# 160 instead of 128 of 512 tokens of an expert layer by rows fetched by index: PE stages of 352 columns, first one-hots on GpSimd

## What is computed

```python
qry = (tb @ w_q).reshape(128, 8, 2, 128)          # tb: RMS-normed tokens
s = einsum('thpd,pkd->thpk', qry, sub_keys)       # 2 x 128 keys
...                                               # top 16 of 16*16 sums, per head
eidx = take_along_axis(cidx, pos)                 # 16 of 16384 experts for each of 8 heads
gates = softmax(top)
z = einsum('thed,td->the', expert_u[eidx], tb)
act = gates * gelu(z)
out = einsum('the,thed->td', act, expert_v[eidx])
```

## Time and profile before

| | us |
|---|---|
| three runs | 4529.89, 4532.38, 4532.43 |
| median | 4532.38 |
| the profiled execution, whole | 4528.72 |
| its span, first to last instruction | 4527.2 |
| PE busy in it | 4451.7 (98%) |
| DVE busy | 3336.6 (74%) |
| DMA, mean | 281 GB/s |

### The profile page before, as it was taken

The page is one execution under the profiler, slowest core; times in us unless marked ns, Lnnn a source line. Parts: engine busy times, 40 slices in busy tenths (PEclk is TensorE's granted clock), DMA queues, the critical chain, the costliest instruction groups (busy, mean ns, idle before and its releaser), DMA issues.

```text
span 4527.2 us, 66430 instructions
## 1 busy us (share of the span) xinstructions
PE 4451.7 (98%) x24985; PEld 4089.4 (90%) x24985; DVE 3336.6 (74%) x4048; ACT 1301.7 (29%) x1217; POOL 712.1 (16%) x742
## 2 busy tenths in 40 slices
PE   8999999999999999999899999999999999999998
PEld 6788878999999788878799999999999999999998
DVE  5767675988888645558878888777746788887886
ACT  4222222222222331222123444322223222322223
POOL 1111111010101200111111112233311111111113
PEclk9999999999999999999999999999999999999999
DMA  6988986888888968898446777898876888888884
GB/s 214 320 288 291 314 280 229 288 286 290 286 289 287 332 229 286 286 322 311 151 141 238 294 287 281 308 354 332 332 262 238 314 319 293 315 316 301 307 290 149
DMA packets 390000, 1272.99 MB, mean 281 GB/s; under 512 B 28288, under 2 KB 204304, under 8 KB 282272
## 3 DMA queue, kind: packets, MB, share of 16 engines
q1 hardware_dynamic: 335872, 940.51, 60.5%
q0 software_dynamic: 54048, 331.51, 19.6%
HBM read 1070.46 MB, written 335.61 MB: 311 GB/s over the span
## 4 chain that ended last, share of the span: by engine, by line
PE 83%; DVE 6%; DMA 5%; issue 3%; SPq 2%; ACT 1%; POOL 1%; DVEq 0%; POOLq 0%; ACTq 0%
PE bank L757 26%; PE bank L758 26%; PE bank L759 26%; DMA u_rows<-u_turned_b 2%; PE bank L981 2%; DMA u_rows<-u_turned_c 1%; SPq L402 1%; DVE w_lo L1424 1%; PE bank L857 1%; DVE u_turned_b L1431 1%; PE bank L864 1%; ACT w_hi L1047 1%; DVE u_turned_c L1431 1%; PE bank L833 1%; POOL cand L674 1%
## 5 line engine op out<-in xcount | busy, mean ns | idle before, releaser
L757 PE MATMUL bank<-x_hi,w_hi 128*128 128x384 f32 (+2 forms) x5760 | 1973.5, 343 | 27.0 <-DVE w_lo L1424 19.7
L758 PE MATMUL bank<-x_lo,w_hi 128*128 128x384 f32 (+2 forms) x5760 | 1966.6, 341 | 0.0
L759 PE MATMUL bank<-x_hi,w_lo 128*128 128x384 f32 (+2 forms) x5760 | 1958.0, 340 | 0.0
L1047 ACT ACTIVATE w_hi<-w_raw 128x2048 fp32r<-128x2048 f32 x432 | 827.2, 1915 | 1859.8 <-PE bank L759 1808.8
L1424 DVE TENSOR_TENSOR w_lo<-w_raw,w_hi 128x2048 fp32r<-128x2048 f32 x432 | 996.0, 2305 | 450.4 <-ACT w_hi L1047 448.1
L757 PEld LDWEIGHTS bank<-x_hi,w_hi 128*128 128x128 f32 x5760 | 1084.6, 188 | 131.9 <-issue 39.2
L759 PEld LDWEIGHTS bank<-x_hi,w_lo 128*128 128x128 f32 x5760 | 1087.6, 189 | 82.4
L758 PEld LDWEIGHTS bank<-x_lo,w_hi 128*128 128x128 f32 x5760 | 1085.2, 188 | 84.7 <-issue 2.6
L757 PE MATMUL bank<-x_hi_o,w_hi 128*128 128x384 f32 x2048 | 684.4, 334 | 0.7 <-DVE w_lo L1424 0.5
L758 PE MATMUL bank<-x_lo_o,w_hi 128*128 128x384 f32 x2048 | 684.1, 334 | 0.0
L759 PE MATMUL bank<-x_hi_o,w_lo 128*128 128x384 f32 x2048 | 684.1, 334 | 0.0
(11 more groups left out here) (284 smaller groups left out, 2726.8 us busy)
## 6 DMA issues: line engine op xcount, KB each, us to landing
v_rows<-v_blocks SPq DMA_DIRECT2D x128, 1024.0 KB, 10.4
w_raw<-u_blocks SPq DMA_DIRECT2D x128, 1024.0 KB
w_raw<-v_blocks SPq DMA_DIRECT2D x128, 1024.0 KB
w_raw<-w_proj SPq DMA_DIRECT2D x112, 1024.0 KB
u_raw_a<-u_blocks SPq DMA_DIRECT2D x99, 1024.0 KB, 8.3
u_rows<-u_turned_a SPq DMA_DIRECT2D x396, 256.0 KB, 5.7
z_scratch<-z_stage POOLq DMA_DIRECT2D x128, 192.0 KB
g_scratch<-g_chunk SPq DMA_DIRECT2D x12, 2048.0 KB, 12.1
```

Source lines behind the costliest of these rows:

```text
L757: pe.matmul(dst, whi, xhi, start=start, stop=False)
L758: pe.matmul(dst, whi, xlo, start=False, stop=False)
L759: return pe.matmul(dst, wlo, xhi, start=False, stop=stop)
L1047: act.activation(WH[s][:, :], RAW[s][:, :], ACT.Copy).then_inc(w_hi, 1)
```

## The change

- The first NT = 352 tokens go densely (N3 = 384 keeps the size of everything else). Every matmul of the U and V stages has 352 columns. z_stage, g, z_group and x_hi_o, x_lo_o shrink likewise. G needs 44 blocks (Z_GATE = 44) instead of 48.
- Tokens 352 to 383 go by pairs too. Their 32 x 128 pairs are laid over the partitions in four groups: partition 32 g + t holds pairs 32 g to 32 g + 31 of token t. So 32 more fetches and dots (ZIX, XRX, ZPX), and 32 more fetches and adds (VIX, GSX), ahead of the old 128: 160 in all (PAIRS).
- Their set-up: 16 more scalings on ACT and 16 transposes on PE in the Q and U stages (X_AT, take_x), an index computation of 12 instructions and a copy (rsX) on DVE ahead of the last table look-up, 12 small DMAs on POOL that spread the indices and gates over the partitions, one more transpose, one more GELU.
- In the V stage the four partial sums of a token have to be added: the first 32 adds are done by block 24, then behind block 25 PE multiplies ACC with a 0/1 matrix sel (16 matmuls, `x_flush`), DVE clears ACC and adds the result to out_sums (`x_flushed`), and the other 128 adds follow over blocks 26 to 119.
- hot_i is made by POOL, as four tensor_scalar of 128 elements for each group (`hot_rows`), with its own semaphore hot_i_rdy. In POOL's order a block's z store comes first, then the next block's hot_rows, then the u_rows.
- dots: 70 over the 44 gate blocks, 90 over the next 62 (to block 121). SP's wait for the last dot stands in front of the last 2 weight blocks instead of the last 8. The Python loops of DVE and POOL are written out.

```diff
-Z_LOOK, Z_GATE, TOK = 16, 48, 8
+Z_LOOK, Z_GATE, TOK = 16, 44, 8
...
-NT = TG * P
+N3 = TG * P
+NX = 32
+XG = P // NX
+XP = P // XG
+NT = N3 - NX
+PAIRS = XP + P
...
-V_FIRST, V_LAST = 1, 119
+X_FIRST, X_LAST, V_FIRST, V_LAST = 1, 24, 26, 119
+X_FLUSH = 25
...
-D_GATE, D_LATE = 9, 9
+D_GATE, D_LAST = 70, NB_E - 7
...
         def dots(n):
+            g = Z_LOOK + Z_GATE
+            upto = lambda m: (D_GATE * (m - Z_LOOK) // Z_GATE if m <= g else
+                              min(PAIRS, D_GATE + (PAIRS - D_GATE) * (m - g) // (D_LAST + 1 - g)))
+            return range(upto(n), upto(n + 1))
...
-            with sp.Fori(0, 26) as i:
+            g_chunk(NT // CH // 2, 0)
+            with sp.Fori(0, 31) as i:
                 z_load(Z_LOOK + 4 + Z_GATE + 2 * i)
...
-            sp.wait_ge(ug_dot, P)
+            sp.wait_ge(ug_dot, PAIRS)
             group_load(sp, 1, 1, zg_first, gg_first)
...
-            with sp.Fori(0, 4) as i:
-                z_load(Z_LOOK + 4 + Z_GATE + 52 + 2 * i)
+            z_load(NB_E - 2)
...
+            def hot_rows(n):
+                for g in range(2):
+                    pool.wait_ge(g_mm, 2 * n + (g + 1))
+                    pool.sem_inc(turns[1], 1)
+                    for q in range(4):
+                        tok = TOK * n + 4 * g + q
+                        o = pool.tensor_scalar(hot_i[g][:, q, :], iota[:, :], IT[:, tok:tok + 1], None, ALU.is_equal)
+                    o.then_inc(hot_i_rdy, 1)
...
+            pool.wait_ge(xi_rdy, 2)
+            for g in range(XG):
+                to, at_ = slice(NX * g, NX * g + NX), slice(XP * g, XP * g + XP)
+                pool.dma_start(ZIX[to, :], ZIT[P - NX:P, at_]).then_inc(xi_ld, 16)
+                pool.dma_start(VIX[to, :], VIT[P - NX:P, at_]).then_inc(xi_ld, 16)
+                pool.dma_start(GSX[to, :], GA[P - NX:P, TG - 1, at_]).then_inc(xi_ld, 16)
...
             for n in range(Z_LOOK, NB_E):
                 z_stores(n)
+                if n + 1 < Z_LOOK + Z_GATE:
+                    hot_rows(n + 1 - Z_LOOK)
                 for p in dots(n):
-                    if p + VSLOT < P:
+                    if p + VSLOT < PAIRS:
                         pool.wait_ge(ug_dot, p + 1)
                         u_row(p + VSLOT)
...
                         pe.wait_ge(hot_rdy, 4 * i + 2 * u + g + 1)
+                        pe.wait_ge(hot_i_rdy, 4 * i + 2 * u + g + 1)
...
+            def x_flush():
+                pe.wait_ge(vg_use, v_uses(XP - 1) + 1)
+                pe.wait_ge(sel_rdy, XG - 1)
+                for k in range(KT):
+                    m = pe.matmul(A[1][:, NX * k:NX * k + NX], ACC[:, P * k:P * k + P], sel[:], start=k == 0, stop=k == KT - 1,
+                                  skip_group_check=True)
+                m.then_inc(ax_rdy, 1)
...
-                        dve.tensor_tensor(hot_i[g][:, :, :], iota[:, :].unsqueeze(1).to_broadcast((P, 4, P)),
-                                          IT[:, ds(TOK * n + 4 * g, 4)].unsqueeze(2).to_broadcast((P, 4, P)), ALU.is_equal)
...
+            def x_flushed():
+
+                dve.wait_ge(ax_rdy, 1)
+                dve.memset(ACC[:, :], 0.0).then_inc(vg_use, 1)
+                o = OUT[:, :, NT:N3]
+                dve.tensor_tensor(o, A[1][:, :].rearrange("p (k t) -> p k t", k=KT), o, ALU.add).then_inc(ax_add, 1)
```

More of the change, by code:

```diff
@@ L225, in encoder_block @@
     HG = place("h_rows", [P, KT, P], F32, r1 + 8 * GJ * NT)
[L226 removed]
+    (OUT, ACC), e13 = lay(r2, [("out_sums", [P, KT, N3], F32), ("v_sums", [P, D], F32)])
     assert e13 <= dd
@@ L530, in _ @@
                       allow_small_or_imprecise_dtypes=True).then_inc(pool_const, 1)
+            pool.wait_ge(pool_const, 3)
+            pool.tensor_tensor(sel[:], ident[:, 0:NX], ident[:, NX:2 * NX], ALU.add).then_inc(sel_rdy, 1)
+            for g in range(2, XG):
+                pool.wait_ge(sel_rdy, g - 1)
+                pool.tensor_tensor(sel[:], sel[:], ident[:, NX * g:NX * g + NX], ALU.add).then_inc(sel_rdy, 1)
             pool.wait_ge(g_row, 2)
@@ L1011, in out_group @@
                         out_block(16 * gg + 8 * par + 2 * m_ + u, u, par)
-            with pe.Fori(0, KEYS // GJ // 2 - 1) as gg:
+            def x_flush():
[5 more added lines that the diff above has]
+                m.then_inc(ax_rdy, 1)
+            for g in range(4):
+                if g < X_FLUSH // 8:
+                    out_group(g // 2, g % 2)
+                else:
+                    pe.wait_ge(x_lo, 80 + 8 * g + 8)
+                    pe.sem_inc(turns[2], 1)
+                    for r in range(8):
+                        out_block(8 * g + r, r % 2, g % 2)
+                        if 8 * g + r == X_FLUSH:
+                            x_flush()
+            with pe.Fori(2, KEYS // GJ // 2 - 1) as gg:
                 for par in range(2):
@@ L1951, in _, with dot @@
-            with dve.Fori(0, 8) as i:
-                for b in range(6):
-                    n = 6 * i + (Z_LOOK + Z_GATE + b)
-                    z_scale(n, b % 2, 8 * n - 8 * (b % 2))
-                    for r in dots(Z_LOOK + Z_GATE + b):
-                        dot(D_LATE * i + r, r % VSLOT, 3 * i + (r // VSLOT + 1))
-            for n in range(Z_LOOK + Z_GATE + 48, NB_E - 2):
+            dve.wait_ge(tr_ev, 4)
+            def dot(p):
+                s = p % VSLOT
+                x, z = (XRX, ZPX[:, p:p + 1]) if p < XP else (XR, ZP[:, p - XP:p - XP + 1])
+                dve.wait_ge(ug_ld[s], 16 * (p // VSLOT) + 16)
+                dve.scalar_tensor_tensor(UG[s][:, :], UG[s][:, :], 1.0, x[:, :, :, :].rearrange("p a k c -> p (a k c)"),
+                                         ALU.mult, ALU.mult, accum_out=z).then_inc(ug_dot, 1)
@@ new lines, in hots @@
+            def hots(n):
+                for g in range(2):
+                    dve.wait_ge(g_mm, 2 * n + (g + 1))
+                    for q in range(4):
+                        tok = TOK * n + 4 * g + q
+                        o = dve.tensor_scalar(hot_j[g][:, q, :], iota[:, :], JT[:, tok:tok + 1], AT[:, tok:tok + 1],
+                                              ALU.is_equal, ALU.mult)
+                    o.then_inc(hot_rdy, 1)
+            for n in range(Z_LOOK, NB_E - 2):
+                if n < Z_LOOK + Z_GATE:
+                    hots(n - Z_LOOK)
@@ L1958, in _ @@
                 z_scale(n, n % 2, 8 * (n - n % 2))
-                for r in dots(n):
-                    dot(r, r % VSLOT, r // VSLOT + 1)
+                for p in dots(n):
+                    dot(p)
             def product(g, par, jj):
```

236 lines of the change are left out of this document (136 added, 100 removed).

## The result

| | us |
|---|---|
| before, measured beside it | 4531.14 (4528.30 to 4532.43) |
| after, four runs | 4573.77 (4571.45 to 4580.61) |
| ratio, 95% interval | 1.0097 [1.0080, 1.0115] |
| predicted | 4435 (4378 to 4510) |
| the profiled execution after: whole, span | 4571.93, 4570.4 |

The account below looks back on a forecast made before the run. The prediction took PE to bound the kernel, with DVE setting blocks 0 to 15. Its terms, 0 - 1 - 39 + 5 - 68 + 6 = -97 us, gave 4528.7 - 97 + 3.7 = 4435 us, range 4378 to 4510.

Parts of the forecast that it names:

- What bounds the kernel, and a column's price: Whole kernel: PE busy 98% of the span; 32 columns less at 0.433 ns save 13.9 ns a matmul.
- Late U blocks: 64 late U blocks fall to 7.76 us each, -39 us, bounds -42 and -20.
- Blocks up to 15 and the end of U: Blocks 0 to 15, set by DVE: 0 (-4 to +5); late weight load at U's end: +5 (0 to +15).
- Gate blocks: Gate stage: 10.6 us a block with PE waiting for one-hots, a gain of 1 us instead of 40.
- the upper of the two bounds: Gate stage: a tensor_scalar with a pointer costs POOL twice the copy, 12.8 us a block, +96.
- Its own signs: Gate stage: DVE busy over 90%, hot_i 0.28 us alone; block of 9.7: turns free; 12 or more: POOL the bound.
- One-hots on POOL cost more than they free: Rival, gate stage: POOL's 8 instructions take turns with DVE's, u_row fetches queue behind; 4570 us at 0.7 each; chance 0.12.
- V blocks: V stage: 7.8 us a block, 128 x 0.53 = -68 us; bounds 7.67 (-84) and 8.2 (-17).
- Nothing is left for a wait: V stage: DVE's work sums to 7.66 us a block where PE wants 7.67.
- bound by DMA or DVE: Rival, V stage: DMA or DVE sets it at 8.2 us a block, 51 less gained, 4486 us; chance 0.15.
- The sign that the prediction had set: V stage: DMA share under 0.9 with PE waiting means the DVE queue's order, not its load, is the cause.
- Flush: V blocks 24 and 25: late adds, 16 matmuls and DVE's clearing cost +6 us, between +2 and +10.

Follow-up runs that it names:

- the cuts: Changed kernel with v_adds over 256 of 2048 columns: 4531.34 us; with every fourth v_row fetch left out: 4543.06; with both: 4508.36.
- the fastest kernel: Changed kernel with all one-hots on DVE, 60 gate dots, late low parts, tiles 6 and 7 together, flush behind V block 26: 4412.10 us.

## Why the prediction was wrong, point by point

- **What bounds the kernel, and a column's price: right.** Late U blocks took 7.68 us (7.76 forecast), PE without a stop; a matmul's pitch was 431.00/2696 = 159.9 ns for 161.5. Even the kernel that was slower as a whole won 46 us there.
- **Blocks up to 15 and the end of U: right** (-2 for 0; the +5 for the end didn't show, 68.3 and 68.0).
- **Gate blocks: the step that failed, +99 for -1.** It said "the two engines take turns, and each of the 8 hot_i costs DVE what it lasts", at 0.28 us each. It put DVE's queue down as the bound. Three things in it were wrong. The price alone is 0.59, the upper of the two bounds that stood there (twice the copy, with 12.8 us for a block; measured 12.75). The loser is POOL and not DVE: the earlier trace rows shows a POOL copy held until just behind lo's end, and that row held the answer; the prediction charged the conflict to DVE instead of asking what eight such delays do to POOL's queue. DVE's back-to-back instructions left POOL so little that eight took up to 13.7 us. Its own signs say so: DVE was to be busy over 90% and was 69%, and "at 12 or more POOL is the bound". That the sum with DVE as the loser and 0.56 us each gives 12.8 is therefore luck. And the clock was not in the sum at all, though the trace of before had a row for it: behind the wait of 4.0 us it fell to 0.50. It cost some 41 us here.
- **The rival had the mechanism.** "One-hots on POOL cost more than they free", with the fetches queued behind, was given 0.12 and 4570 us at 0.7 us each. That 4574 was measured is luck. By its own price (35 us for each 0.1 us above 0.56) 0.7 us give 13.9 a block and 4581, not 4570; measured were 1.04 us and 12.75 a block, and the V stage missed as well. Its argument against, "the copy takes 0.28", is the row that misled: same shape, another instruction.
- **V blocks: 8.21 for 7.8, near the bound of 8.2.** "Nothing is left for a wait" was seen and then given only 0.13 us. DVE was busy for 0.87 of these blocks and DMA for 0.88, and the cuts show that each alone was enough to make PE wait. The rival "bound by DMA or DVE" named 8.2 and both causes; it was right here. The sign that the prediction had set (DMA under 0.9 with PE waiting means the order of DVE's queue and not its load) came up, and was half right: the place of the adds was worth about 40 us in the fastest kernel, but the load counts too, since shorter adds alone took 22 us off these blocks.
- **Flush: +13 for +6.** Blocks 24 to 27 took 45.8 us, and four blocks of 8.21 are 32.8. The wait for the last adds was 4.5 us (3 forecast); most of the rest is the lower clock behind it (0.85 in the mean from 3698 to 3744 us). With the adds done earlier and no wait the four take 35.1 us, and +2 is left.
- The Trainium skill ("SBUF — State Buffer", section "Who interferes with whom") says that a VectorE instruction with two SBUF inputs contends with a GpSimd instruction that reads SBUF, that the port pair they share is an exclusive lock, and that issue order decides who blocks. The trace agrees for GpSimd (0.59 us alone, eight in 13.63) and hardly for VectorE in this stage (2.31 us for a dot in the mean, 2.29 before); the measurement decides: the block was all but one-sided here. The prediction took from the rule that the move "saves DVE nothing" and gave the 2.16 us copy as agreement, but that copy is GpSimd waiting. DVE was relieved: busy for 386 us of the stage, 424 with hot_i back on it.
- **Slips in its sums.** Two groups of four hot_j are 2.2 us and not 2.1, so its gate block is 10.7; that changes nothing. The chances follow as 0.88, 0.03 and 0.09 from the cases, where it says 0.87, 0.04 and 0.09.
